# Expert weights in loads of seven slabs instead of three, in the same ring of 21 slabs

## The reference

```python
def swiglu(h, w_gate_up, w_down):
    gt, up = jnp.split(h @ w_gate_up, 2, axis=-1)
    return (jax.nn.silu(gt) * up) @ w_down

# moe_swiglu: each token takes its top 2 of 8 experts
for e in range(N_EXPERTS):
    y = y + combine[:, e:e + 1] * swiglu(t, w_gate_up[e], w_down[e])
```

## Time and profile before

| | |
|---|---|
| time, median of 3 runs (lowest to highest) | 1577.01 us (1576.56 to 1577.22) |
| the profiled execution's own time | 1576.93 us |
| its span, first to last instruction | 1575.1 us |
| PE busy | 1529.7 us, 97% |
| DVE, ACT, POOL busy | 521.0, 457.3, 90.5 us |
| moved by DMAs | 485.62 MB |
| expert loads of three slabs | 97 of 3072 KB, median 28.1 us from issue to landing |
| expert loads of one slab | 45 of 1024 KB, median 16.7 us |

### The profile page before, as it was taken

How to read it: one execution, slowest core, us unless ns; L and a number is a source line. 1 busy time by engine, 2 the same in 40 slices (tenths; PEclk the granted TensorE clock), 3 DMA queues, 4 the chain that set the end, 5 groups by cost and what they waited for, 6 DMA issues and landing times.

```text
span 1575.1 us, 31274 instructions
## 1 busy us (share of the span) xinstructions
PE 1529.7 (97%) x14130; PEld 967.4 (61%) x14130; DVE 521.0 (33%) x619; ACT 457.3 (29%) x598; POOL 90.5 (6%) x128
## 2 busy tenths in 40 slices
PE   8999999999999999999999999999999999999877
PEld 7788888788888888888345453363433533534324
DVE  5755575655567565665200101001010010000101
ACT  5557653544455666462000000000000000000000
POOL 5211100000002110001000000000000000000000
PEclk9999999999999999998999999999999999999999
DMA  7555455666655454777999999999999999999995
GB/s 270 182 155 160 148 174 160 215 190 189 188 177 190 150 177 144 252 285 288 391 392 378 426 426 428 424 429 426 425 427 429 425 426 426 418 416 427 424 431 244
DMA packets 82305, 485.62 MB, mean 308 GB/s; under 512 B 9920, under 2 KB 12032, under 8 KB 64000
## 3 DMA queue, kind: packets, MB, share of 16 engines
q1 hardware_dynamic: 79120, 474.67, 77.5%
q0 software_dynamic: 3056, 8.99, 1.6%
HBM read 481.53 MB, written 2.10 MB: 307 GB/s over the span
## 4 chain that ended last, share of the span: by engine, by line
PE 86%; DMA 9%; DVE 2%; POOL 2%; issue 1%; ACT 0%; SPq 0%; DVEq 0%; POOLq 0%
PE pa L2060 27%; PE ps L2060 19%; PE pa L1931 12%; PE pa L1933 12%; PE pa L1932 12%; DMA exp_raw<-in_moe_slabs 8%; PE ps L2338 1%; DMA w_raw<-in_w_mem_kv 1%; DVE w_lo L1253 1%; POOL hrs L748 1%; POOL head_gains L677 0%; PE ps L2308 0%; PE ps L1858 0%; DVE hs L1808 0%; ACT hs L1215 0%
## 5 line engine op out<-in xcount | busy, mean ns | idle before, releaser
L2060 PE MATMUL pa<-exp_raw,xf 128*32 128x512 f32 (+1 forms) x5120 | 498.0, 541 | 25.4 <-DMA exp_raw<-in_moe_slabs 15.8
L2060 PEld LDWEIGHTS pa<-exp_raw,xf 128*32 128x32 f32 x5120 | 162.3, 110 | 318.6 <-issue 259.8
L1253 DVE TENSOR_TENSOR w_lo<-w_raw,w_hi 128x1024 fp32r<-128x1024 f32 x226 | 274.3, 1232 | 122.3 <-ACT w_hi L883 113.2
L883 ACT ACTIVATE w_hi<-w_raw 128x1024 fp32r<-128x1024 f32 (+1 forms) x228 | 236.9, 1053 | 147.3 <-PE pa L1933 145.4
L2060 PE MATMUL ps<-exp_raw,hf 128*32 128x256 f32 x4480 | 248.2, 379 | 5.2 <-DMA exp_raw<-in_moe_slabs 5.2
L1931 PE MATMUL pa<-w_hi,r 128*128 128x512 f32 x600 | 239.7, 399 | 1.8 <-DVE r L1288 1.7
L1933 PE MATMUL pa<-w_hi,r 128*128 128x512 f32 x600 | 234.0, 390 | 0.0
L1932 PE MATMUL pa<-w_lo,r 128*128 128x512 f32 x600 | 233.9, 390 | 0.0
L2060 PEld LDWEIGHTS ps<-exp_raw,hf 128*32 128x32 f32 x4480 | 144.9, 110 | 108.6 <-issue 12.7
L1808 DVE TENSOR_TENSOR hs<-pa,hs 128x768 f32<-128x768 f32 (+3 forms) x32 | 23.7, 742 | 344.7 <-ACT hs L1215 344.7
L1931 PEld LDWEIGHTS pa<-w_hi,r 128*128 128x128 f32 x600 | 112.6, 188 | 29.1 <-issue 3.2
(11 more groups left out here) (274 smaller groups left out, 863.5 us busy)
## 6 DMA issues: line engine op xcount, KB each, us to landing
exp_raw<-in_moe_slabs SPq DMA_DIRECT2D x97, 3072.0 KB, 28.1
w_raw<-in_w_in SPq DMA_DIRECT2D x104, 512.0 KB, 4.3
exp_raw<-in_moe_slabs SPq DMA_DIRECT2D x45, 1024.0 KB, 16.7
w_raw<-in_ff_w_gate_up SPq DMA_DIRECT2D x44, 512.0 KB, 4.6
w_raw<-in_ff_w_down SPq DMA_DIRECT2D x22, 512.0 KB, 4.0
w_raw<-in_w_mem_kv SPq DMA_DIRECT2D x16, 512.0 KB, 5.4
w_raw<-in_w_out SPq DMA_DIRECT2D x16, 512.0 KB, 4.3
w_raw<-in_w_br_sb SPq DMA_DIRECT2D x8, 512.0 KB, 3.6
```

Of the source, the lines that this page charges most:

```text
L883: act.activation(dst, raw, ACT.Copy).then_inc(hi_ready, 1)
L1253: dve.tensor_tensor(dst, raw, hi.bitcast(F32), ALU.subtract)\
L2060: return pe.matmul(dst, a, b, start=start, stop=stop, skip_group_check=True)
```

## The change

`LOAD` becomes 7. Everything else follows from it: the ring of 21 slabs is three places of seven; a load brings seven slabs, 56 KB for each partition in one run, 7 MB in all, and is issued when PE has used the seventh slab of the place; PE begins on its slabs when all seven have landed; and `END` is 35, so that the last seven slabs of each expert are loaded singly. The list in `first_slabs` stays as it is. The layout in HBM is made with the same constant, so seven slabs now lie side by side for each partition.

```diff
 EXP_SLAB = 2048
-EXP_RAW, LOAD = 21, 3
+EXP_RAW, LOAD = 21, 7
```

## The result

| | before | after |
|---|---|---|
| time, median (lowest to highest) | 1577.12 us (1576.56 to 1577.42) | 1606.09 us (1603.05 to 1607.67) |
| profiled execution | 1576.93 us | 1605.08 us |
| ratio after / before | | 1.0181 (1.0169 to 1.0192) |

The account below looks back on a forecast made before the run. PE (804 us) and the DMAs (805 us) were taken as balanced, so idle DMA time is paid at the end. 1576.93 + 21 for PE's waits + 2 for the clock = 1600 us; own range 1593 to 1606, whole range 1587 to 1611.

Parts of the forecast that it names:

- Which engine is the limit, by expert: Experts' part: wide experts are PE's (17 us in hand), few experts the DMAs' (21 us short), balanced over all.
- Longer runs gain a little: All loads of seven: 56 KB runs take 2.423 us a slab, 16.96 for seven; gain 1.9 us.
- Rival 3: 56 KB runs move slower, or the token gather and code loads come off worse behind longer packets: 1609; 10%.
- The 56 us: Win if each of 121 DMAs, now 93, paid about 2.0 us fixed; set aside because loads land 7.31 us apart.
- Later issue, DMA idle time: Loads wait for seven used slabs: DMAs idle 18.3 us by slab 63, 27.4 in all against 9.9 before.
- my corrected theory: Set before the run with sevens in the first expert alone: idle time where PE limits only moves; +4 us, 1581.
- Later use, three waits: First slabs of the third, fifth and eighth expert: a load's first slab waits for six others; PE waits 9, 8.3, 8.5.
- The end: Last expert: last landing 1581, PE ends 6.3 us after, 26.5 us for 14 slabs; the last seven takes the singles' gain.
- Sum of waits: PE's waits over the whole kernel: 42.2 us against 21.0 before, +21.2.
- The clock: PE's clock may fall to half after the three waits of 8 to 9 us: 2 us, bounds 0 and 8.
- rival 4: The clock falls at each long wait and is paid in full: +28, 1606; 12%.
- Rival 1: Faster, the queue is deep enough: only the runs (-2) and the singles at the end (-3) count, 1572; 5%.

## Why the prediction was right, step by step

- *Which engine is the limit, by expert*: right. Few experts are the DMAs', wide experts PE's, and few experts with sevens carry two thirds of the loss. The last 29 us, behind the last load of seven, are PE's.
- *Longer runs gain a little*: right in sign and size for the rate (16.9 us for seven slabs, 16.96 forecast). Against the same schedule in single slabs the gain was 0.034 us a slab, half of the 0.064 that the rates give. Rival 3 fell for the loads; its other half, a gather that is slower behind long loads, came true (23.7 us to land instead of 13.7), and nothing waited for it. The 56 us that the prediction works out from the Trainium skill and sets aside rest on a figure that the page DMA: Bandwidth & Descriptors gives in the section Anatomy of one DMA, for DMAs issued by GpSimd; the loads here are SyncE's.
- *Later issue, DMA idle time*: right in place (757 to 862, and expert 5) and near in size: 27 us forecast, 17.5 more than before. The first window and that of expert 5 show about 13 and 11, which is 9 and 11 more. The sentence that idle time is paid at the end was borne out by late issue alone (12.6 us idle, 13.9 paid) and by the single slabs at the start, 6.8 us with those at the end. It was too strong for the two loads of the first expert, which cost 3.1 us of the 8 that the prediction gave the start, and my corrected theory, by which idle time while PE is the limit only moves it, fits that kernel (4 expected) but not late issue.
- *Later use, three waits*: 7.91, 8.37 and 8.46 measured against 9, 8.3 and 8.5. The waits were as forecast because both sides moved: the first load of expert 7 landed at 1496.4, 6.7 us later than the 1489.7 forecast, and PE came to it nearly as late (1488.0, forecast 1482.3).
- *The end*: right that the last load of seven takes back what single slabs win. PE ends 11.2 us after the last landing, 6.3 were forecast. Of the 4.9 us between, 2.6 are PE's, by the half clock from 1566 (29.1 us for 14 slabs instead of 26.5), and some 2 are that the last slab landed 17.9 us after the last load of seven and not 19.8. The half clock from 1531 is not in it, since PE waited for loads again at 1549 and 1566.
- *Sum of waits*: 39.7 against 42.2 forecast.
- *The clock*: the term that was mis-sized, as an item of PE's time. I took 2 us from bounds of 0 to 8 and counted three waits. There were five, two of them the waits of 3.1 and 4.2 us in the last expert, and 23 us of work at half clock, 11.5 us. With waits 2.5 below forecast and a start 1.7 earlier this adds up to 1605 instead of 1600. As a cause it is shown only in part: filler in the three long waits gave back 3.5 us by the medians and nothing in the profiled pair. The measured time is that of rival 4 (1606), but its mechanism, the half clock paid in full at each long wait, is not borne out; that the number agrees is partly luck. Why the first load of expert 7 landed 6.7 us later than forecast stays open; a PE that is late at half clock and so frees places late is one way to it, and was not tried by itself.
- *Rival 1* (deep queue) was half true in the sense that a late load finds a queue for most of the time; the two stretches where it does not, and the late use at the first slab of experts 2, 4 and 7, decided.

## What to carry to other kernels

The size of a load is three decisions at once: how long the runs are, how late the load is issued, and how late its first byte may be used. With a ring of fixed size, late issue and late use cost more together than apart. Read the queue in front of the DMAs (time from issue to landing) along the kernel: where it is short, load in small pieces; where the consumer runs on the heels of the landings, the first load must be small; elsewhere large loads were free here. Idle time of the DMAs counts where they and the consumer are balanced over the whole, as here: 12.6 us of it in the first wide expert cost 13.9. The loads that cause it may be the next expert's, since they are issued a ring's length (here half an expert) before they are used.

## What the runs showed of the hardware

- Runs of 24 KB, 8 KB and 56 KB for each partition took 7.31 us for three slabs, 2.49 for one and 16.9 for seven, 430, 421 and 434 GB/s behind a full queue: above 24 KB there is hardly anything left to gain. The size of the DMA grew with the run, so the two are not apart.
- Long runs hold up other traffic. The gather of an expert's tokens, from GpSimd's queue, takes 13.7 us (median, issue to landing) in the kernel before, 23.7 in the changed one and 9.2 in the kernel with late issue and late use in 8 KB runs. It is no matter of idle DMAs, since with neither, where they are full, it takes 9.3. The rows below are that tile's, of the changed kernel and of the one with both and short runs. It had time to spare here (the first is issued at 769 and used at 849); a kernel that waits for such a gather would not.

The changed kernel:

```profile
DMA to landing us min/median/max: 15.3/23.7/24.9
```

The kernel with late issue and late use, 8 KB runs:

```profile
DMA to landing us min/median/max: 8.5/9.2/10.2
```

- The clock fell also with waits on loads of 3.1 and 4.2 us in the changed kernel, with half clock for 5 to 6 us of work after each; of the waits on loads in the kernel before, up to 2.6 us, none was followed by a fall, nor was one of 2.7 us at 1549 in the changed kernel. The length of the last wait alone does not decide: in the kernel before, the fall at 969 (the second of rows 9) came behind a wait of 1.5 us for VectorE, with a few small products before it.
